# Score and value matmuls of two attention heads on alternating halves of the TensorE array

## The chip, the cores and the metric

The kernel runs on one core of one Trainium2 chip. The metric is the device time of the whole program in microseconds, from its first to its last instruction with the launch around it; lower is better. The chip has a TensorE (matrix engine, 128 x 128 array, "PE" in the profile, its weight loads "PEld"), VectorE ("DVE"), ScalarE ("ACT"), GpSimd ("POOL") and SyncE ("SP", which here issues DMA transfers).

## The reference

A two-layer decoder trunk on one sequence of 512 tokens with 1024 channels, float32. The part that matters here is the token mixing between two feed-forward blocks:

```python
h = rms_norm(x, mix_norm[i])
z = h @ w_in[i]
qkv_shape = (Bn, S, A_N_GROUPS, A_HEADS_PER_GROUP, HEAD_DIM)
q = z[..., Q_OFF:K_OFF].reshape(qkv_shape)
...
y_a = dilated_attention_mixture(q, k, v)
...
gates = jax.nn.sigmoid(z[..., G_OFF:] + b_gate[i]).reshape(Bn, S, N_BRANCH, D)
merged = (gates[:, :, 0] * (y_a @ w_proj_a[i])
          + gates[:, :, 1] * (y_b @ w_proj_b[i])
          + gates[:, :, 2] * (y_c @ w_proj_c[i]))
x = x + merged @ w_out[i]
```

There are 3 groups of 4 heads with 64 channels each. `dilated_attention_mixture` is a masked softmax attention per group, with the groups of one head slot mixed by their softmax denominators, which is one softmax over the keys of all three. Group 0 of a head looks back 128 tokens, group 1 at every 4th and group 2 at every 16th token. The kernel takes the tokens of one residue modulo 4 together, so one piece of attention is one head and one residue: 128 queries against 512 + 128 + 128 = 768 keys.

## The kernel before

**Projections.** Channels lie on the partitions, tokens in the free dimension. Each float32 product with a weight is made of three fp32r products, high by high, high by low and low by high. A "unit" is one block of a weight, 1024 rows by 256 columns. SyncE loads it into `raw`, ScalarE copies its high part to `w_hi` (L737), VectorE subtracts to get `w_lo` (L1030). There are two slots of each, so a unit is split while TensorE works on the one before it. One unit is 48 matmuls of 128 x 128 weights and 512 columns (2 column halves x 8 blocks x 3 products) into two banks of a PSUM pair, `psum0` or `psum1`. `columns` (L433) makes the units in a row.

**Attention phase.** It lies once in each layer, between the units of q and k for heads 0 and 1 and the merge of the three branches. It has 16 pieces of attention (4 heads x 4 residues) and, between them, 6 whole units: three for q and k of heads 2 and 3, three for the first three gates. The order is written out by hand in a loop over 18 slots: in a slot TensorE does the scores of the next piece, 8 projection matmuls (`part`, L444), the transposes of this piece, 8 more projection matmuls, and the values of this piece. Slots 0 and 9 have no piece of their own; before the scores in slot 9, TensorE waits until VectorE has taken the unit that held q and k of heads 2 and 3.

- `scores` (L619): three plain float32 matmuls of 64 rows (one head's channels, partitions 0 to 63 or 64 to 127) by 128 columns of weights against 512, 128 and 128 keys, into `side0`. The trace shows each float32 matmul as two, each with its own load.
- VectorE adds the mask and takes the row maximum (L1340, L1344), ScalarE takes the exponential (L941), VectorE divides (L1349, L1350).
- `transposes` (L629): six blocks of 128 x 128 into `side1`, copied by ScalarE to `pT` (L963).
- `values` (L641): six float32 matmuls of 128 rows by 64 columns of weights against 128 columns, summed into partitions 0 to 63 or 64 to 127 of the last 128 columns of `side1`. ScalarE copies the high part (`head_hi`, L926), VectorE subtracts the low part (`head_lo`, L1329).

All 4 residues of head 0 come first, then those of head 1, and so on, so that pieces in a row use the same half of the array.

**Merge.** `project` multiplies ya (2 blocks), yb (4) and yc (4) by 256 columns of their weights, in the order a, b, c; VectorE multiplies each with its gate and adds (L1392 to L1403). Three gate units of the next 256 columns stand before each following `project`.

Of the kernel before, what the change touches and what calls it, by code (L numbers as in the profile page):

```python
# [18 lines left out]
F32 = mybir.dt.float32  # L19
# [56 lines left out]
def trunk(nc, x, ffn1_norm, ffn1_w_gate, ffn1_w_up, ffn1_w_down, mix_norm, w_in, b_gate, b_ln_g,  # L76
# [16 lines left out]
    ATT = HEADS * RES  # L93
    KEYS = S + 2 * P
# [5 lines left out]
    EV0, EV1 = 47, 47  # L100
# [4 lines left out]
    with ExitStack() as ctx:  # L105
# [48 lines left out]
        pT = at("pT", M + 42 * KB_, KEYS)  # L154
# [52 lines left out]
        unit_done = sem("unit_done")  # L207
        evacuated = [sem(f"evacuated{s}") for s in range(2)]
# [43 lines left out]
        SLOTS = 18  # L252
# [7 lines left out]
        OUT_BANKS = (2, 1, 0, 1)  # L260

        def attended(s):

            if s in (0, 9) or not 0 < s < SLOTS:
                return None
            return s - 1 if s < 9 else s - 2
# [6 lines left out]
        def _(sp):  # L273
# [40 lines left out]
            with rounds(sp, DEPTH, counts, split_made=UNITS_PER_LAYER) as layer:  # L314
# [83 lines left out]
        def _(pe):  # L398
# [39 lines left out]
            def part(dst, w, x_hi, x_lo, q0, q1):  # L438

                whi, wlo = w  # L440
                for q in range(q0, q1):
                    c, k, n = q // (3 * KD), q // 3 % KD, q % 3
                    l, r = ((whi, x_hi), (whi, x_lo), (wlo, x_hi))[n]
                    mm = nc.tensor.matmul(dst[:, c * S:(c + 1) * S], l[:, k * UNIT_N + c * P:k * UNIT_N + (c + 1) * P],  # L444
                                          r[:, k * S:(k + 1) * S], start=(k == 0 and n == 0), stop=(k == KD - 1 and n == 2))
                return mm

# [70 lines left out]
            with rounds(pe, DEPTH, counts, unit=UNITS_PER_LAYER, ev0=EV0, ev1=EV1,  # L518
                        sv0=8 + ATT, sv1=4, h=3 * D_PAIRS, acc=3 * (1 + KD), act=2 * FF_UNITS, w_sT=1, pooled=4,
                        vb=1, p=ATT, pT=ATT, head=ATT, y=2, merged=D_PAIRS) as layer:  # L520
# [88 lines left out]
                def scores(n):  # L609
                    j, r = divmod(n, RES)  # L610
                    rows_ = slice((j % 2) * HEAD_DIM, (j % 2 + 1) * HEAD_DIM)
                    t = qk[j // 2]
                    o = begin_side(0)
                    col = 0
                    for g in range(GROUPS):
                        q, k = g * S + r * P, (GROUPS + g) * S
                        keys = t[rows_, k:k + S] if g == 0 else t[rows_, k + r * P:k + (r + 1) * P]
                        width = S if g == 0 else P
                        mm = nc.tensor.matmul(o[:, col:col + width], t[rows_, q:q + P], keys, start=True, stop=True)  # L619
                        col += width  # L620
                    mm.then_inc(side_done[0], 1)

                def transposes(n):

                    pe.wait_ge(p_made, counts["p"].next())

                    pe.wait_ge(head_made, counts["head"].next())
                    for c in range(KEYS // P):
                        mm = nc.tensor.transpose(side[1][:, c * P:(c + 1) * P], p_tile[n % 2][:, c * P:(c + 1) * P], ident[:, :])  # L629
                    mm.then_inc(pT_written, 1)  # L630

                def values(n):
                    j, r = divmod(n, RES)

                    pe.wait_ge(pT_made, counts["pT"].next())
                    out_rows = slice((j % 2) * HEAD_DIM, (j % 2 + 1) * HEAD_DIM)
                    o = side[1][out_rows, KEYS:KEYS + P]
                    for c in range(KEYS // P):
                        g, t = (0, c) if c < TILES else (c - TILES + 1, r)
                        col = t * A_WIDTH + g * A_OUT + j * HEAD_DIM  # L640
                        mm = nc.tensor.matmul(o, v[:, col:col + HEAD_DIM], pT[:, c * P:(c + 1) * P],  # L641
                                              start=(c == 0), stop=(c == KEYS // P - 1))
                    mm.then_inc(head_done, 1)

                pair_of = (0, 1, 0, 1, 0, 1)
                STEP = 3 * 2 * KD // 6
                for s in range(SLOTS):
                    m, third = divmod(s, 3)
                    this, after = attended(s), attended(s + 1)
                    if third == 0:  # L650
                        o = begin(pair_of[m])
                        w = unit()
                    if this is not None and after is not None:
                        scores(after)

                    start, end = 2 * STEP * third, 2 * STEP * (third + 1)
                    before, between = (STEP, STEP) if s < SLOTS - 1 else (STEP // 2, STEP - 2)
                    part(o, w, h_hi, h_lo, start, start + before)
                    if this is None:
                        if s == 0:  # L660

                            pe.wait_ge(side_evacuated[1], counts["sv1"].now(1))

                        pe.wait_ge(evacuated[1 - pair_of[m]], counts[f"ev{1 - pair_of[m]}"].now(1))
                        scores(after)
                    else:
                        transposes(this)
                    mm = part(o, w, h_hi, h_lo, start + before, start + before + between)
                    if third == 2 and s < SLOTS - 1:
                        mm.then_inc(unit_done, 1)  # L670
                    if this is not None:
                        values(this)
                part(o, w, h_hi, h_lo, start + before + between, end).then_inc(unit_done, 1)

                def project():
                    columns(begin(0), unit(), ya_hi, ya_lo, range(KA), True, True).then_inc(unit_done, 1)
                    columns(begin(1), unit(), yb_hi, yb_lo, range(KB), True, True).then_inc(unit_done, 1)
                    columns(begin(0), unit(), yc_hi, yc_lo, range(KB), True, True).then_inc(unit_done, 1)  # L680
                pe.wait_ge(head_made, counts["head"].now(1))
                pe.wait_ge(y_ready, counts["y"].next(2))
                project()
                with rounds(pe, D_PAIRS - 1, counts, unit=6, ev0=3, ev1=3):
                    for s in (1, 0, 1):
                        columns(begin(s), unit(), h_hi, h_lo, range(KD), True, True).then_inc(unit_done, 1)
                    project()
# [36 lines left out]
        def _(act):  # L724
# [105 lines left out]
            with rounds(act, DEPTH, counts, unit=UNITS_PER_LAYER, raw0=8 * UNITS_PER_LAYER + 16 * 2,  # L830
                        raw1=8 * UNITS_PER_LAYER + 16 * 3, ev0=EV0, ev1=EV1, se0=8 + ATT, act=2 * FF_UNITS,
                        sd0=7 + ATT, sd1=4, ln=1, yb=2, neg=ATT, pT_written=ATT, head=ATT, merged=D_PAIRS) as layer:
# [84 lines left out]
                counts["sd0"].next(ATT)  # L917
# [3 lines left out]
                def head_hi(n):  # L921
                    j, r = divmod(n, RES)
                    rows_ = slice((j % 2) * HEAD_DIM, (j % 2 + 1) * HEAD_DIM)
                    act.wait_ge(head_done, counts["head"].next())
                    dst = ya_hi[rows_, (j // 2) * S:(j // 2 + 1) * S].rearrange("p (i r) -> p r i", r=RES)[:, r, :]
                    nc.scalar.activation(dst, side[1][rows_, KEYS:KEYS + P],  # L926
                                         ACT.Copy).then_inc(ya_hi_made, 1)
# [10 lines left out]
                def exponential(n):  # L938

                    act.wait_ge(neg_max_made, counts["neg"].next())  # L940
                    nc.scalar.activation(p_tile[n % 2][:, :], p_tile[n % 2][:, :], ACT.Exp, bias=neg_max[:, n % 2:n % 2 + 1],  # L941
                                         accum_out=row_sum[:, n % 2:n % 2 + 1]).then_inc(exp_made, 1)

                bias_col = T_BGATE + layer * (3 * KD)
                next_unit = [dict(parts=2), dict(parts=2), {}, {}, {}, dict(k=KA)]
                for s in range(SLOTS):
                    m, third = divmod(s, 3)
                    if attended(s - 1) is not None:
                        head_hi(attended(s - 1))
                    if third == 0:  # L950
                        if m > 0:
                            counts["unit"].next()
                            if m - 1 < 3:
                                counts[f"ev{(m - 1) % 2}"].next()
                        split(**next_unit[m])
                    if third == 1 and m > 3:
                        sigmoids(m - 4, (m - 1) % 2, bias_col)
                    if third == 1 and m > 3:

                        exponential(attended(s + 1))  # L960
                    if attended(s) is not None:
                        act.wait_ge(pT_written, counts["pT_written"].next())
# [495 lines left out]
```

## Time and profile before

| | |
|---|---|
| median of 3 runs | 2417.64 us (2417.22 to 2418.68) |
| the profiled execution's own time | 2416.66 us |
| its span, first to last instruction | 2414.9 us |
| mean granted TensorE clock | 0.997 of full speed |
| busy: TensorE, its loads, VectorE, ScalarE, GpSimd | 2394.2, 1969.6, 1095.0, 716.6, 30.5 us |
| attention phase of layer 0, from its first projection matmul to the last one | 525.59 to 655.24 us |
| attention phase of layer 1 begins | 1715.33 us |

The busy time says which engine is full. The chain that ended last says, step by step, which instruction each next one waited for. The groups by line give how many of a kind there are and how long one takes; matmuls are pipelined, so the mean of one is longer than the distance between two starts, and the distance is what counts.

### The profile page before, as it was taken

The page shows a single profiled execution, that of the slowest core. Times are in us where ns is not written, and L with a number is a line of the kernel's source. Part 1 is how long each engine was busy: PE and PEld are TensorE (multiplying, and loading weights), DVE is VectorE, ACT ScalarE, POOL GpSimd, SP SyncE. Part 2 cuts the span into 40 slices and gives each one's busy share as a digit, 9 for nine tenths or more (in the row PEclk, how much of TensorE's full clock was granted, in tenths as well). Part 3 has the DMA queues.
Part 4 walks back from the last instruction along what each step waited for, and adds up shares of the span by engine and source line. Part 5 has one row for each costly group of instructions (what it writes and reads, how often), then busy time and mean ns, then how long its engine had stood idle before and what let it go on. Part 6 is the DMA issues. An engine that isn't in the chain of part 4 may idle for free.

```text
span 2414.9 us, 27466 instructions
## 1 busy us (share of the span) xinstructions
PE 2394.2 (99%) x11021; PEld 1969.6 (82%) x11021; DVE 1095.0 (45%) x1045; ACT 716.6 (30%) x665; POOL 30.5 (1%) x58
## 2 busy tenths in 40 slices
PE   7999999999999999999999999999999999999999
PEld 6888888887788888888888888888777888888887
DVE  7444435544454554443344443365544445544433
ACT  4222223323422332222232222232334223322222
POOL 4000000000000000000000000000000000000000
PEclk9999999999999999999999999999999999999999
DMA  4333223321132323322332332332312233232221
GB/s 141 94 97 104 81 98 122 95 81 40 40 104 87 114 89 102 104 89 95 96 101 91 104 100 84 96 116 79 88 31 66 83 109 109 91 104 91 96 96 65
DMA packets 229756, 221.81 MB, mean 92 GB/s; under 512 B 4161, under 2 KB 227505, under 8 KB 229681
## 3 DMA queue, kind: packets, MB, share of 16 engines
q1 hardware_dynamic: 225696, 215.29, 28.4%
q10 hardware_dynamic: 3984, 5.51, 0.7%
q8 instruction: 48, 0.79, 0.1%
q14 instruction: 28, 0.22, 0.0%
HBM read 218.69 MB, written 2.10 MB: 91 GB/s over the span
## 4 chain that ended last, share of the span: by engine, by line
PE 97%; ACT 1%; DVE 1%; issue 0%; DMA 0%; ACTq 0%; DVEq 0%
PE psum L433 83%; PE psum L444 5%; PE side L641 2%; PE psum L561 2%; PE side L619 2%; PE side L433 1%; PE psum L453 1%; PE side L629 1%; DVE acc L1087 0%; PE side L571 0%; PE side L543 0%; DMA x_in<-in_x_dram 0%; ACT gate L934 0%; PE side L582 0%; ACT L941 0%
## 5 line engine op out<-in xcount | busy, mean ns | idle before, releaser
L433 PE MATMUL psum<-h_hi,w_hi 128*128 128x512 f32 x1984 | 776.0, 391 | 8.7 <-DVE w_lo L1030 8.5
L433 PE MATMUL psum<-h_lo,w_hi 128*128 128x512 f32 x1984 | 772.8, 390 | 0.0
L433 PE MATMUL psum<-h_hi,w_lo 128*128 128x512 f32 x1984 | 772.7, 389 | 0.0
L1030 DVE TENSOR_TENSOR w_lo<-raw,w_hi 128x2048 fp32r<-128x2048 f32 (+2 forms) x224 | 470.9, 2102 | 338.5 <-ACT w_hi L737 337.8
L737 ACT ACTIVATE w_hi<-raw 128x2048 fp32r<-128x2048 f32 (+2 forms) x224 | 393.8, 1758 | 601.9 <-PE psum L433 578.1
L433 PEld LDWEIGHTS psum<-h_hi,w_hi 128*128 128x128 f32 x1984 | 373.0, 188 | 88.5 <-issue 9.2
L433 PEld LDWEIGHTS psum<-h_hi,w_lo 128*128 128x128 f32 x1984 | 373.0, 188 | 77.9
L433 PEld LDWEIGHTS psum<-h_lo,w_hi 128*128 128x128 f32 x1984 | 373.1, 188 | 77.7 <-issue 1.2
L433 PE MATMUL psum<-act_hi,w_hi 128*128 128x512 f32 x704 | 273.9, 389 | 0.0
L433 PE MATMUL psum<-act_lo,w_hi 128*128 128x512 f32 x704 | 273.9, 389 | 0.0
L433 PE MATMUL psum<-act_hi,w_lo 128*128 128x512 f32 x704 | 273.9, 389 | 0.0
L793 ACT ACTIVATE act_hi<-us 128x1024 f32 (+1 forms) x44 | 46.7, 1061 | 455.0 <-DVE us L1118 455.0
L1052 DVE TENSOR_TENSOR us<-psum,rstd 128x1024 f32<-128x1024 f32 x44 | 53.9, 1225 | 276.5 <-PE psum L433 276.5
L433 PEld LDWEIGHTS psum<-act_hi,w_lo 128*128 128x128 f32 x704 | 132.2, 188 | 27.5
L433 PEld LDWEIGHTS psum<-act_lo,w_hi 128*128 128x128 f32 x704 | 132.2, 188 | 27.5
L433 PEld LDWEIGHTS psum<-act_hi,w_hi 128*128 128x128 f32 x704 | 132.2, 188 | 27.2
L1052 DVE TENSOR_TENSOR gs<-psum,rstd 128x1024 f32<-128x1024 f32 x44 | 53.9, 1225 | 119.4 <-PE psum L433 118.9
L1120 DVE TENSOR_TENSOR act_lo<-us,act_hi 128x1024 f32 (+1 forms) x44 | 53.9, 1226 | 58.7 <-ACT act_hi L793 58.7
L755 ACT ACTIVATE us<-xT 128x1024 f32<-128x1024 f32 x24 | 25.4, 1059 | 185.1 <-DVE xT L1065 185.1
L444 PE MATMUL psum<-h_hi,w_hi 128*128 128x512 f32 x192 | 77.8, 405 | 0.0
L444 PE MATMUL psum<-h_hi,w_lo 128*128 128x512 f32 x192 | 77.7, 405 | 0.0
L444 PE MATMUL psum<-h_lo,w_hi 128*128 128x512 f32 x192 | 77.4, 403 | 0.0
(185 smaller groups left out, 1942.4 us busy)
## 6 DMA issues: line engine op xcount, KB each, us to landing
raw<-in_ffn_w_gate_dram SPq DMA_DIRECT2D x44, 1024.0 KB, 5.3
raw<-in_ffn_w_up_dram SPq DMA_DIRECT2D x44, 1024.0 KB, 5.3
raw<-in_w_in_dram SPq DMA_DIRECT2D x42, 1024.0 KB, 5.3
raw<-in_ffn_w_down_dram SPq DMA_DIRECT2D x32, 1024.0 KB, 4.9
raw<-in_ffn_w_down_dram SPq DMA_DIRECT2D x16, 768.0 KB, 4.2
raw<-in_w_in_dram SPq DMA_DIRECT2D x24, 512.0 KB, 4.4
raw<-in_w_out_dram SPq DMA_DIRECT2D x8, 1024.0 KB, 5.0
raw<-in_w_proj_b_dram SPq DMA_DIRECT2D x8, 512.0 KB, 3.4
```

What stands on the lines that cost most here:

```text
L433: mm = nc.tensor.matmul(dst[:, c * S:(c + 1) * S], l[:, a], r[:, b], start=first and k == ks[0] and n == 0, stop=last and k == ks[-1] and ...
L444: mm = nc.tensor.matmul(dst[:, c * S:(c + 1) * S], l[:, k * UNIT_N + c * P:k * UNIT_N + (c + 1) * P], r[:, k * S:(k + 1) * S], start=(k == ...
L453: mm = nc.tensor.matmul(o, l[:, k * P:(k + 1) * P], r[:, k * S:(k + 1) * S], start=(k == 0 and n == 0), stop=(k == KD - 1 and n == 2))
L561: mm = nc.tensor.matmul(d, l[:, k * S + t * P:k * S + (t + 1) * P], r[:, b], start=(k == 0 and m == 0), stop=(k == KD - 1 and m == 2))
L619: mm = nc.tensor.matmul(o[:, col:col + width], t[rows_, q:q + P], keys, start=True, stop=True)
L641: mm = nc.tensor.matmul(o, v[:, col:col + HEAD_DIM], pT[:, c * P:(c + 1) * P], start=(c == 0), stop=(c == KEYS // P - 1))
L737: nc.scalar.activation(w_hi[s][:, 0:k * n], raw[s][:, 0:k * n], ACT.Copy).then_inc(hi_made, 1)
L755: nc.scalar.activation(sq[:, :], pair(xT, d), ACT.Square).then_inc(sq_made, 1)
L793: nc.scalar.activation(pair(act_hi, i), us[:, :], ACT.Copy).then_inc(act_hi_made, 1)
L1030: nc.vector.tensor_tensor(w_lo[s][:, a], raw[s][:, a], w_hi[s][:, a].bitcast(F32), ALU.subtract).then_inc(split_made, 1)
L1052: return nc.vector.tensor_tensor(dst, two(psum[s][:, :]), rstd2, ALU.mult)
L1120: nc.vector.tensor_tensor(pair(act_lo, i), us[:, :], pair(act_hi, i).bitcast(F32), ALU.subtract).then_inc(act_ready, 1)
```

## The change

- The 16 pieces become 8 pairs: heads 0 and 1 (then 2 and 3) of one residue. `score_pair` issues the three score matmuls of both heads in turn: rows 0 to 63 into `side0`, rows 64 to 127 into `psum1`, which the phase no longer needs for projections. `value_pair` issues the six value matmuls of both heads in turn, to partitions 0 to 63 and 64 to 127 of the same columns of `side1`, with two tiles `pT`.
- `turn_pair` transposes the first head into `side1` and the second into `side0`; ScalarE copies both.
- All six units go through `psum0`, a half (24 matmuls, one bank) at a time; VectorE takes a half as soon as it is done (`take_half`). The places of the scores and of the transposes in the stream of 288 projection matmuls are two tables. The values of a pair follow on the scores of the next pair.
- `head_hi` and `head_lo` take both heads at once (128 partitions, 8 times a layer instead of 16).
- In the merge the order is b, a, c, with the PSUM pairs exchanged, and TensorE waits for the last head's output only before the a unit. SyncE loads the weights in that order.

The core of the diff:

```diff
+        SCORES_AT = (10, 48, 86, 124, 162, 194, 226, 258)
+        TURNS_AT = (38, 76, 114, 152, 185, 217, 249, 281)
-                    for w in (w_proj_a, w_proj_b, w_proj_c):
+                    for w in (w_proj_b, w_proj_a, w_proj_c):
...
+                def project_to(end):
+                    for q in range(stream["at"], end):
+                        h, k, n = q // (3 * KD), q // 3 % KD, q % 3
+                        c = h % 2
+                        if q % (3 * KD) == 0:
+                            pe.wait_ge(evacuated[0], free + max(h - 1, 0))
+                            if c == 0:
+                                stream["w"] = unit()
...
+                def score_pair(n):
+                    jp, r = divmod(n, RES)
+                    t = qk[jp]
+                    outs = (begin_side(0), begin(1))
+                    if n == RES:
+                        pe.wait_ge(evacuated[0], free + 6)
                     for g in range(GROUPS):
...
+                        for b in range(2):
+                            mm = nc.tensor.matmul(outs[b][:, col:col + k1 - k0], t[rows_of(b), q:q + P], t[rows_of(b), k0:k1],
+                                                  start=True, stop=True)
...
+                def value_pair(n):
+                    jp, r = divmod(n, RES)
+                    pe.wait_ge(pT_made, counts["pT"].next())
+                    pe.wait_ge(side_evacuated[0], counts["sv0"].now(1 if n == PAIRS - 1 else 0))
                     pe.wait_ge(head_made, counts["head"].next())
                     for c in range(KEYS // P):
                         g, t = (0, c) if c < TILES else (c - TILES + 1, r)
+                        for b in range(2):
+                            col = t * A_WIDTH + g * A_OUT + (2 * jp + b) * HEAD_DIM
+                            mm = nc.tensor.matmul(side[1][rows_of(b), KEYS:KEYS + P], v[:, col:col + HEAD_DIM],
+                                                  pT[b][:, c * P:(c + 1) * P], start=(c == 0), stop=(c == KEYS // P - 1))
...
+                for n in range(PAIRS):
+                    project_to(SCORES_AT[n])
+                    score_pair(n)
+                    if n > 0:
+                        value_pair(n - 1)
+                    project_to(TURNS_AT[n])
+                    turn_pair(n)
+                project_to(PHASE)
+                value_pair(PAIRS - 1)
...
+                for n in range(PAIRS):
+                    if n == 0:
+                        step(parts=2)
+                    if n > 0:
+                        head_hi(n - 1)
+                    if n == 1:
+                        step(parts=2)
+                    if n == 5:
+                        step()
+                    for b in range(2):
+                        exponential(b)
+                    if n in (2, 3):
+                        step()
+                    if n == 6:
+                        step(KB)
+                    take_turned()
+                    if n in (5, 6):
+                        counts["ev0"].next()
+                        sigmoids(n - 5, 0, bias_col)
```

TensorE in the attention phase before: the end of one slot's projection matmuls, the values of a piece, the scores of the next (`qk_87`: q and k of heads 0 and 1), and on.

```order
L444 MATMUL psum<-h_lo,w_hi_55 128x512
L641 MATMUL side<-pT,v 64x128 [waits pT_made]
L641 MATMUL side<-pT,v 64x128 x5
L410 REGISTER_ALU
L619 MATMUL side<-qk_87 128x512 [waits side_evacuated0]
L619 MATMUL side<-qk_87 128x128 x2
L444 MATMUL psum<-h_hi,w_lo_57 128x512
```

The same place now: the scores of one pair, behind them the values of the pair before (`pT_94` and `pT_95` are the two heads' tiles), then projection matmuls.

```order
L405 REGISTER_ALU [waits side_evacuated0]
L634 MATMUL side<-qk_87 128x512 [waits evacuated1]
L634 MATMUL psum<-qk_87 128x512
L634 MATMUL side<-qk_87 128x128
L634 MATMUL psum<-qk_87 128x128
L634 MATMUL side<-qk_87 128x128
L634 MATMUL psum<-qk_87 128x128
L663 MATMUL side<-pT_94,v 64x128 [waits head_made,side_evacuated0,pT_made]
L663 MATMUL side<-pT_95,v 64x128
L663 MATMUL side<-pT_94,v 64x128
L663 MATMUL side<-pT_95,v 64x128
```

What moved: heads alternate from one matmul to the next, and the values stand behind the scores instead of ahead of them. Eight value matmuls more follow.

ScalarE now, at the sixth pair: the split of a unit (`w_hi`) ahead of both exponentials, the two copies of the transposed tiles, then the sigmoids of a gate with their table load, ahead of the next pair's output and exponentials.

```order
L927 ACTIVATE ya_hi<-side 128x128 [waits head_done]
L736 REGISTER_ALU
L738 REGISTER_ALU [waits raw_loaded0]
L739 ACTIVATE w_hi_54<-raw_52 128x2048 [waits unit_done]
L940 REGISTER_ALU
L941 ACTIVATE p_tile_92,small<-p_tile_92,small 128x768 [waits neg_max_made]
L940 REGISTER_ALU
L941 ACTIVATE p_tile_93,small<-p_tile_93,small 128x768 [waits neg_max_made]
L946 ACTIVATE pT_94<-side 128x768 [waits pT_written]
L948 ACTIVATE pT_95<-side 128x768 [waits pT_written]
L932 REGISTER_ALU
L934 ISA [waits evacuated0]
```

Before, the exponential of a piece stood behind the copy of the piece before it; now both exponentials of a pair stand ahead of the copies of their own pair.

## Rows read from the trace of the kernel before

**Rows 1.** the page: busy time of each engine over the run

```profile
PE 2394.2 (99%) x11021; PEld 1969.6 (82%) x11021; DVE 1095.0 (45%) x1045; ACT 716.6 (30%) x665; POOL 30.5 (1%) x58
```

**Rows 2.** the page: the chain that ended last, by engine and line

```profile
PE psum L433 83%; PE psum L444 5%; PE side L641 2%; PE psum L561 2%; PE side L619 2%; PE side L433 1%; PE psum L453 1%; PE side L629 1%; DVE acc L1087 0%; PE side L571 0%; PE side L543 0%; DMA x_in<-in_x_dram 0%; ACT gate L934 0%; PE side L582 0%; ACT L941 0%
```

**Rows 3.** stretches: TensorE in the two attention phases, us, busy (count), clock

```profile
525.60:653.64 128.04, 126.65 (x667) 1.00 0.14 44
1715.33:1843.40 128.07, 126.67 (x668) 1.00 0.15 44
```

**Rows 4.** chain through one slot: start us, us, engine, tile, line

```profile
538.42 1.50 PE side L619 x6
539.92 2.04 PE psum L444 x8
541.96 0.66 PE side L629 x6
542.61 1.84 PE psum L444 x8
544.45 1.46 PE side L641 x12
```

**Rows 5.** the chain where layer 0's phase begins, turns and ends

```profile
525.59 1.81 PE psum L444 x8
...
590.23 2.01 DVE qk L1309 x2
...
655.24 64.94 PE psum L433 x286
```

**Rows 6.** groups of layer 0's phase: busy us, mean ns | idle before

```profile
L444 PE MATMUL psum<-h_hi,w_hi 128*128 128x512 f32 x96 | 38.9, 405 | 0.0
...
L619 PE MATMUL side<-qk 64*128 64x128 f32 (+1 forms) x96 | 25.1, 394 | 1.0 <-DVE qk L1309 1.0
L641 PE MATMUL side<-pT,v 128*64 128x128 f32 x192 | 24.4, 277 | 0.4 <-ACT pT L963 0.3
...
L926 ACT ACTIVATE ya_hi<-side 64x128 fp32r<-64x128 f32 x16 | 6.3, 392 | 26.6 <-PE side L641 26.6
```

**Rows 7.** waits of TensorE there: us in total, times, longest

```profile
PE side L619 <- DVE qk L1309: 1.0, 1, 1.0
PE side L641 <- ACT pT L963: 0.3, 1, 0.3
```

**Rows 8.** time order, TensorE in a value group (1, 3, 12 passes)

```profile
544.38 0.32 PE L641 MATMUL side<-pT,v 128*64 128x128 f32 x1
...
544.38 0.54 PE L641 MATMUL side<-pT,v 128*64 128x128 f32 x3
...
544.38 1.52 PE L641 MATMUL side<-pT,v 128*64 128x128 f32 x12
```

**Rows 9.** time order, loads of a score group, first projection matmul behind

```profile
546.37 0.19 PEld L619 LDWEIGHTS side<-qk 64*128 64x128 f32 x1 [0.24 <-issue]
...
546.80 0.30 PEld L619 LDWEIGHTS side<-qk 64*128 64x128 f32 x2 [0.24 <-issue]
...
612.39 0.50 PE L444 MATMUL psum<-h_hi,w_hi 128*128 128x512 f32 x1
```

**Rows 10.** time order, VectorE and ScalarE behind a score group

```profile
554.93 0.95 DVE L1340 CUSTOM_DVE_ANT_0 p_tile<-side,masks 128x768 f32<-128x768 f32 x1 [0.71 <-issue]
...
559.58 0.62 DVE L1350 TENSOR_SCALAR p_tile<-p_tile,small 128x768 f32<-128x768 f32 x1
...
557.62 0.81 ACT L963 ACTIVATE pT<-side 128x768 f32<-128x768 f32 x1 [3.80 <-PE side L629]
558.33 0.93 ACT L941 ACTIVATE p_tile<-p_tile,small 128x768 f32<-128x768 f32 x1
```

**Rows 11.** time order, ScalarE: a split, a table load

```profile
611.18 1.92 ACT L737 ACTIVATE w_hi<-raw 128x2048 fp32r<-128x2048 f32 x1
...
618.89 1.28 ACT L934 ACT_TABLE_LOAD   x1
```

More of the change, by code:

```diff
@@ L93, in trunk @@
     ATT = HEADS * RES
+    PAIRS = ATT // 2
     KEYS = S + 2 * P
@@ L436, in columns @@
                 return mm
[L438 to L446, printed above, removed]
             def one_column(o, w):
@@ new lines, in turn_pair @@
+                def turn_pair(n):
+                    pe.wait_ge(p_made, counts["p"].next())
+                    if n == 0:
+                        pe.wait_ge(side_evacuated[1], counts["sv1"].now(1))
+                    for c in range(KEYS // P):
+                        mm = nc.tensor.transpose(side[1][:, c * P:(c + 1) * P], p_tile[0][:, c * P:(c + 1) * P], ident[:, :])
+                    mm.then_inc(pT_written, 1)
+                    pe.wait_ge(p_made, counts["p"].next())
+                    o = begin_side(0)
+                    for c in range(KEYS // P):
+                        mm = nc.tensor.transpose(o[:, c * P:(c + 1) * P], p_tile[1][:, c * P:(c + 1) * P], ident[:, :])
+                    mm.then_inc(pT_written, 1)
@@ L632, in values @@
[L632 to L638, printed above, removed]
-                        g, t = (0, c) if c < TILES else (c - TILES + 1, r)
[L640 to L672, printed above, removed]
@@ new lines, in _, with project @@
+                for n in range(PAIRS):
[7 more added lines that the diff above has]
+                value_pair(PAIRS - 1)
+                def project(last_head=False):
+                    columns(begin(1), unit(), yb_hi, yb_lo, range(KB), True, True).then_inc(unit_done, 1)
+                    if last_head:
+                        pe.wait_ge(head_made, counts["head"].now(1))
@@ L678, in project @@
                     columns(begin(0), unit(), ya_hi, ya_lo, range(KA), True, True).then_inc(unit_done, 1)
-                    columns(begin(1), unit(), yb_hi, yb_lo, range(KB), True, True).then_inc(unit_done, 1)
-                    columns(begin(0), unit(), yc_hi, yc_lo, range(KB), True, True).then_inc(unit_done, 1)
-                pe.wait_ge(head_made, counts["head"].now(1))
+                    columns(begin(1), unit(), yc_hi, yc_lo, range(KB), True, True).then_inc(unit_done, 1)
                 pe.wait_ge(y_ready, counts["y"].next(2))
-                project()
+                project(True)
@@ L921, in head_hi @@
                 def head_hi(n):
[L922 to L927, printed above, removed]
+                    jp, r = divmod(n, RES)
+                    act.wait_ge(head_done, counts["head"].next(2))
+                    dst = ya_hi[:, jp * S:(jp + 1) * S].rearrange("p (i r) -> p r i", r=RES)[:, r, :]
+                    nc.scalar.activation(dst, side[1][:, KEYS:KEYS + P], ACT.Copy).then_inc(ya_hi_made, 1)
                 def sigmoids(g, s, col):
@@ L946, in _ @@
[L946 to L962, printed above, removed]
-                        nc.scalar.activation(pT[:, :], side[1][:, 0:KEYS], ACT.Copy).then_inc(pT_made, 1)
-                    if attended(s + 1) is not None and not (third == 1 and m > 3):
-                        exponential(attended(s + 1))
@@ L966, in _, with take_turned @@
-                head_hi(ATT - 1)
-                counts["unit"].next()
+                    nc.scalar.activation(p_tile[b][:, :], p_tile[b][:, :], ACT.Exp, bias=neg_max[:, b:b + 1],
+                                         accum_out=row_sum[:, b:b + 1]).then_inc(exp_made, 1)
+                def take_turned():
+                    act.wait_ge(pT_written, counts["pT_written"].next())
+                    nc.scalar.activation(pT[0][:, :], side[1][:, 0:KEYS], ACT.Copy).then_inc(pT_made, 1)
+                    act.wait_ge(pT_written, counts["pT_written"].next())
+                    nc.scalar.activation(pT[1][:, :], side[0][:, 0:KEYS], ACT.Copy).then_inc(side_evacuated[0], 1)
@@ L1383, in _ @@
-                head_lo(ATT - 1)
-                done()
-                take_gate(2, 1)
+                        evac(0, take_qk(1, QK_UNITS[m][c], 0, c))
+                    else:
+                        evac(0, nc.vector.tensor_tensor(gate[m - 3][:, c * S:(c + 1) * S], psum[0][:, c * S:(c + 1) * S],
+                                                        rstd[:, :], ALU.mult))
+                for n in range(PAIRS):
+                    score_max(n)
+                    if n > 0:
+                        head_lo(n - 1)
+                    normalise(0)
+                    normalise(1)
+                    if n < 4:
+                        take_half((0, 2, 3, 5)[n])
+                        split()
+                        if n in (0, 2):
+                            take_half((1, None, 4)[n])
+                    elif n in (4, 7):
+                        take_half(6 if n == 4 else 10)
+                        take_half(7 if n == 4 else 11)
+                    elif n == 5:
+                        split()
+                        take_half(8)
+                    else:
+                        take_half(9)
+                        split(KB)
```

170 lines of the change are left out of this document (83 added, 87 removed).

## The prediction

> **What bounds the kernel now.** I read first the busy times of the page, then its chain of work, then the stretches of the attention phases, one slot of the chain, the groups and waits of that phase, and last single instructions in order of time. TensorE is busy 99% of the span [rows 1], and 83% of the chain are its projection matmuls outside the attention phase, which the change leaves alone [rows 2]. So time can only come from TensorE's own work or from its few idle gaps. In the two attention phases it is busy for 126.65 and 126.67 us of 128 at a granted clock of 1.00, which is the 2.4 GHz level [rows 3]. VectorE and ScalarE work there too, but TensorE waits for them only twice in layer 0: 1.0 us for q and k in slot 9 and 0.3 us for a copy behind a sigmoid [rows 7].
>
> One slot takes 7.50 us: scores 1.50, 8 projections 2.04, transposes 0.66, 8 projections 1.84, values 1.46 [rows 4]. Two readings matter. First, 8 projections cost 0.20 us more behind scores than behind transposes: TensorE pays about 0.2 us when it changes between the whole array and half of it. It pays the like in front of values and between values and scores: twelve value passes take 1.52 us from first start to last end, three take 0.54 us, so the passes are (1.52 - 0.54) / 9 = 0.109 us apart [rows 8], 1.31 us for twelve, and 1.46 us holds 0.15 us of change. In the scores the long passes are 546.80 - 546.37 = 0.43 us apart [rows 9]; with two long and four short passes of 0.11 us that is 1.30 us, and 1.50 holds 0.20 us of change. Second, every pass of a group now uses the same half of the array, and each load is issued when the pass ahead of it starts (the two load rows are those 0.43 us apart [rows 9]), never two ahead.
>
> **The change, part by part**, per layer. The stretch before goes from 525.59 to 655.24 us [rows 5], 129.65 us: 16 scores x 1.50 = 24.0, 16 values x 1.46 = 23.4, 16 transposes x 0.66 = 10.6, 288 projections (three kinds of 96 [rows 6]) as 36 eights, half at 2.04 and half at 1.84, = 69.8, waits 1.3; 129.1 in all, 0.5 us unassigned.
>
> *Without any overlap*, the new order costs: 288 projections x 0.230 (1.84 / 8) = 66.2; 8 changes back behind the values x 0.20 = 1.6; 16 transposes = 10.6; 8 score pairs x (1.50 + 1.30) = 22.4, since the second head needs no change; 8 value pairs x (1.46 + 1.31) = 22.2. Sum 123.0, so 6.6 us less per layer, 13.3 us in two. This counts the old waits as gone: the 1.0 us because the first scores of heads 2 and 3 stand at projection 162 while the last of their halves is done at 144, 18 x 0.23 = 4.1 us earlier, against 2.01 us for both halves of a unit [rows 5]; the 0.3 us because the sigmoids no longer stand ahead of a copy.
>
> *Overlap of the two halves.* No row of before shows two halves at work at once, so I bound it. The floor of the gain is nothing. The other end: a pass of one head runs together with the preceding head's second pass. Each float32 matmul is two passes, and those two use the same half, so they can't overlap each other. A score pair then takes 3 long and 4 short slots, 3 x 0.43 + 4 x 0.11 = 1.73 us in place of 4 x 0.43 + 8 x 0.11 = 2.60; a value pair takes 13 slots of 0.109 in place of 24, 1.42 in place of 2.62. That is 2.07 us per pair and 33.1 us over 16 pairs. A middle case: the load of the other half isn't issued until the pass ahead of it has started, as all loads in the trace. A load that nothing covers costs about 0.10 us for 128 columns (the first projection behind scores is 0.50 us long, its group's mean is 0.405 [rows 6, 9]) and 0.05 us for 64 columns (first value pass 0.32 against a mean of 0.277 [rows 6, 8]). Stepping through the passes with 0.11 and 0.055, a score pair takes 2.04 us and a value pair 6 x (2 x 0.109 + 2 x 0.055) = 1.97 us: 1.21 us per pair, 19.4 us in all. The trace can't tell these two apart, because the loads it shows go to the half whose spare weights are already taken; I take their middle, 26 us.
>
> The Trainium skill (TensorE: Matmul & The Clock Gate, Part 3, the mechanism) says that a weight load overlaps matmuls in flight only when the row group differs. Our rows speak against the strict form: value loads use all rows and still start with the pass ahead. By the rule the score pair gets its full overlap and the value pair gets none, and the sum would be the second rival's below.
>
> *Other engines.* The mask, maximum, exponential and division are as many as before. Behind the end of a score pair (e) VectorE needs 0.95 us per head plus the negation, so the second maximum is ready at about e + 2.4. ScalarE must first copy the previous pair's output, after the values (about e + 2.1, then 0.39 us [rows 6]); two exponentials of 0.93 us bring e + 4.5, and the division of 0.62 us e + 5.3 [rows 10]. TensorE reaches the transposes only after 23 projections, 5.3 us, at about e + 7.4. The cover is 2 us. A split of 1.92 us ahead of the exponentials (second and sixth pair) or a table load of 1.28 us (seventh, eighth) [rows 11] uses it nearly up, but the second head's tile is needed 0.66 us later still. The two copies of 0.81 us [rows 10] start while the second half of the transposes runs and end about 1.2 us behind it; 9 projections give 2.1 us. If this cover is gone, each late pair puts its lateness on TensorE directly. Taking halves instead of units, one copy and one subtraction per pair instead of two, all lie beside TensorE. SyncE issues the same loads, two in another order. In the merge the matmul count is the same and TensorE never waits in it before; the new order lets the last head's output arrive during the b unit, which I count within the 0.5 us above.
>
> **Sum.** 13.3 + 26.2 = 39.5 us off the profiled execution's 2416.66 us (span 2414.9 and 1.8 around it) is 2377.2; the median of the runs is 1.0 us above that execution, so **2378 us**. The ends of the overlap give 2371 and 2385.
>
> **The rivals.**
> 1. *The halves don't overlap at all* (the change does not do what it says for float32). For it: nothing in the trace shows overlap. Against: the halves share no rows or columns and write different banks or partitions. Only the 13.3 us stay: 2404 us. Chance 0.13.
> 2. *Only the scores overlap*, by 0.87 us x 16 = 13.9 us: value loads for the other half wait, since both use all rows. Against: value loads already run beside passes. 2417.6 - 13.3 - 13.9 = 2390 us. Chance 0.12. It is what the Trainium skill's rule above (the same page and section) would give.
> 3. *Waits take the gain back.* Without overlap, 13.3 / 16 = 0.83 us of lateness per pair at the transposes brings the old time; the covers above speak against more than a few such pairs. 2415 to 2418 us. Chance 0.04.
> 4. *Slower: alternating costs what a change of the array costs.* If going from one half to the other drained TensorE as the change to the whole array does, 0.20 us, a pair with 5 alternations in the scores and 11 in the values would pay 3.2 us, 16 pairs 51 us: 2404 + 51 = 2455 us. It decides from 13.3 / 256 = 0.05 us per alternation. For it: before never alternates within a group. Against: both halves are the same shape of array, and the changes that the rows price are all between shapes. Chance 0.05.
>
> **How the numbers follow.** The overlap in both kinds has 0.66 and spans 2371 to 2385; with a few us of unassigned time on either side 2366 is the low end. Main case and rival 2 are 0.78, so the range must reach rival 1 at 2404. A measurement of this kernel tells 0.2%, about 5 us, from no change: faster by more holds the main case and rivals 1 and 2, 0.91; within it rival 3, 0.04; slower rival 4, 0.05.
>
> **What would show it.** In the profile after, the attention phase should last about 110 us (129.65 - 6.6 - 16.5 = 106.5 at full overlap, 113 with loads one ahead, 123 with none). In order of time, a score pair's first pass of the second head should start before the first head's second pass ends; value passes should stand about 0.06 to 0.08 us apart instead of 0.109. The 0.2 us behind values should be there 8 times. Waits of TensorE for p_tile or pT of over 1 us in all would show the cover wrong; passes further apart than 0.109 us, rival 4. A clock below 1.00 in the phase would be a thing I did not foresee.

## The result, and the profile after

| | before | changed |
|---|---|---|
| median | 2418.16 us (2417.22 to 2418.83, 4 runs) | 2363.05 us (2362.69 to 2363.96, 4 runs) |
| span of the profiled execution | 2414.9 us | 2362.2 us |
| TensorE busy | 2394.2 us | 2344.6 us |
| attention phase of layer 0 | 525.59 to 655.24, 129.65 us | 526.80 to 628.35, 101.55 us |

The ratio of the two is 0.9773, 95% interval 0.9756 to 0.979: 55 us faster. The four times of before are the three of the first table and one more. The prediction was 2378 us, faster, in a range from 2366 to 2404 us. The direction was right, the gain was 40% larger than forecast and the time lies 3 us below the range.

The page of the changed kernel, busy times and granted clock:

```profile
PE 2344.6 (99%) x11021; PEld 1939.8 (82%) x11021; DVE 1090.0 (46%) x1035; ACT 707.8 (30%) x649; POOL 27.9 (1%) x58
...
PEclk9999999999999999999999999999999999999999
```

The stretches of TensorE in both attention phases, changed kernel (us, busy (count), clock, DMA share, GB/s):

```profile
526.80:628.35 101.55, 101.55 (x673) 1.00 0.18 55
1689.29:1790.84 101.55, 101.55 (x674) 1.00 0.18 55
```

Before, the phase took 129.65 us in layer 0 [rows 5] and 129.66 us in layer 1 (1715.33 to 1844.99 in the chain). Both are now 28.1 us shorter. The clock is still full, and the profile shows no wait of TensorE in them: the 1.3 us of [rows 7] are gone.

The chain of the changed kernel through the end of one pair and the next, to hold against [rows 4]:

```profile
540.77 0.62 PE side L634
541.40 0.01 PE psum L634
541.40 0.42 PE side L634
...
542.28 1.46 PE side L663 x24
543.74 6.59 PE psum L616 x28
550.32 0.66 PE side L645 x6
```

The values of two heads, 24 passes, take 1.46 us, as long as the 12 passes of one head before. The scores of two heads go from 540.77 to 542.28, 1.51 us (1.50 in other pairs), as long as those of one head before. So both heads ran at the same time, from the first pass to the last. Single instructions show it. Time order on TensorE in the first part of that score group, changed kernel (start us, us):

```profile
540.70 0.69 PE L634 MATMUL side<-qk 64*128 64x512 f32 x1
540.71 0.69 PE L634 MATMUL psum<-qk 64*128 64x512 f32 x1
541.24 0.59 PE L634 MATMUL side<-qk 64*128 64x512 f32 x1
541.24 0.59 PE L634 MATMUL psum<-qk 64*128 64x512 f32 x1
541.67 0.27 PE L634 MATMUL side<-qk 64*128 64x128 f32 x1
541.67 0.27 PE L634 MATMUL psum<-qk 64*128 64x128 f32 x1
```

`side` is the first head, `psum` the second. Within one head the second pass starts 0.54 us behind the first and the third 0.43 us behind the second (540.70, 541.24, 541.67), as one head alone does, and the other head's pass starts within 0.01 us of each. The loads too run together, the same stretch with the loads shown:

```profile
541.24 0.19 PEld L634 LDWEIGHTS side<-qk 64*128 64x128 f32 x1 [0.23 <-issue]
...
541.25 0.19 PEld L634 LDWEIGHTS psum<-qk 64*128 64x128 f32 x1
```

### The profile page after: what moved, and what is told of

It is laid out like the page before. It is cut to its first block, busy times and chain, and to the rows that moved or that the text cites. A ratio compares the mean times of both kernels' runs of the same rounds, so it can differ in the third digit from the quotient of the medians.

```text
span 2362.2 us, 27568 instructions
## 1 busy us (share of the span) xinstructions
PE 2344.6 (99%) x11021; PEld 1939.8 (82%) x11021; DVE 1090.0 (46%) x1035; ACT 707.8 (30%) x649; POOL 27.9 (1%) x58
## 4 chain that ended last, share of the span: by engine, by line
PE 98%; DVE 1%; ACT 0%; DMA 0%; issue 0%; ACTq 0%; DVEq 0%
PE psum L432 84%; PE psum L616 6%; PE psum L550 2%; PE side L634 1%; PE side L663 1%; PE side L432 1%; PE psum L442 1%; PE side L650 0%; PE side L645 0%; DVE acc L1094 0%; PE side L560 0%; PE side L532 0%; DMA x_in<-in_x_dram 0%; PE side L571 0%; DVE h_lo L1085 0%; PE side L455 0%
```

## The experiments

Ten kernels were timed in three groups, each with the kernel before beside them. It took 2417.82 us beside the first group (scores in blocks, values in blocks, same rows, values two and two), 2416.76 beside the second (values three and three, little overlap, values apart, wait first) and 2417.09 beside the last (mixed merge order, and the changed kernel again, 2362.69). The first group is compared with the changed kernel's 2363.05 us. In the second the changed kernel did not run; 55.1 and 54.4 us less than before, the two differences that were measured, put it at 2361.7 to 2362.4 us. Differences there are taken from 2362.4 and can be 0.7 us larger. Each diff is against the changed kernel.

**Scores in blocks**

```diff
-                    for g in range(GROUPS):
+                    for b in range(2):
+                        for g in range(GROUPS):
...
-                        for b in range(2):
```

> The changed kernel with the score matmuls of a pair in blocks: three of the first head, then three of the second; nothing else moved. Theory A (TensorE starts matmuls in issue order and two neighbours on different halves run side by side, both passes of each): only the last matmul of the first head has a neighbour on the other half, so a score pair costs 0.86 + 0.22 + 1.30 = 2.38 us in place of 1.30, 1.08 us more; 16 pairs 17.3 us, 2380 us in all. Theory B (TensorE looks past a blocked matmul, and the second head's matmuls overtake): no change, 2363 us. Theory C (the gain did not come from overlap but from the other moves): no change, 2363 us.

Measured: 2378.66 us, 15.6 us more than the changed kernel. That is near theory A, and theories B and C are out as they were put. But the single instructions contradict A's first words, that TensorE starts matmuls in issue order. Time order on TensorE in a score group of this kernel (`x3` are three passes in a row):

```profile
540.93 1.23 PE L634 MATMUL side<-qk 64*128 64x512 f32 x3
541.90 0.69 PE L634 MATMUL psum<-qk 64*128 64x512 f32 x1
542.00 0.49 PE L634 MATMUL side<-qk 64*128 64x128 f32 x3
542.43 1.03 PE L634 MATMUL psum<-qk 64*128 64x512 f32 x5
```

In the program all six passes of the first head (`side`) stand ahead of the second head's (`psum`). Yet after three of them a pass of the second head starts, and the last three of the first head only start behind it, from 542.00. So TensorE does not start matmuls strictly in the program's order: a pass whose half is free went ahead of three waiting passes of the other half. The block's price follows: the group takes 541.00 to 543.46 in the chain, 2.46 us in place of 1.50, and 16 x 0.96 = 15.4 us. It is also the sum of the two long passes that the second head starts behind the first, 2 x 0.43 us, and of the 0.10 us of its first load, which nothing covers: its second pass starts 0.53 us behind its first (541.90, 542.43) instead of 0.43.

```profile
541.00 1.16 PE side L634 x3
542.16 0.11 PE psum L634
542.27 0.22 PE side L634 x2
542.50 0.97 PE psum L634 x5
543.46 1.46 PE side L663 x24
```

**Values in blocks**

```diff
-                    for c in range(KEYS // P):
-                        g, t = (0, c) if c < TILES else (c - TILES + 1, r)
-                        for b in range(2):
+                    for b in range(2):
+                        for c in range(KEYS // P):
+                            g, t = (0, c) if c < TILES else (c - TILES + 1, r)
```

> The changed kernel with the value matmuls of a pair in blocks, six of the first head and then six of the second. Theory A (issue order, neighbours on different halves side by side): 11 slots of 2 x 0.109 us in place of 6, 1.09 us more per pair, 17.4 us over 16 pairs, 2380.5 us. Theory B (the second head's overtake) and theory C (no overlap behind the gain): 2363 us.

Measured: 2378.41 us, 15.4 us more. The chain of this kernel has the value pair at 2.39 us:

```profile
541.20 2.39 PE side L663 x24
```

That is 0.93 us more than 1.46. The names of the tiles don't tell the heads apart here, but the starts do: 0.109 us apart up to the ninth pass at 542.05, and the next one already at 542.06. The passes under way at 542.22 and at 542.33 on TensorE, the start of the oldest in front:

```profile
542.05 0.44 PE L663 MATMUL side<-pT,v 128*64 128x128 f32 x4
542.06 0.54 PE L663 MATMUL side<-pT,v 128*64 128x128 f32 x5
```

So the second head starts beside the first head's ninth pass, ahead of the last three, just as in the scores. It is eight passes late, 8 x 0.109 = 0.87 us, and its first load, which nothing covers, adds 0.05 us. Theory A had it start beside the eleventh, 1.09 us late, and so came out 2 us too high.

**Same rows for both heads**

```diff
-                            mm = nc.tensor.matmul(outs[b][:, col:col + k1 - k0], t[rows_of(b), q:q + P], t[rows_of(b), k0:k1],
+                            mm = nc.tensor.matmul(outs[b][:, col:col + k1 - k0], t[rows_of(0), q:q + P], t[rows_of(0), k0:k1],
```

> The changed kernel, but the second head's scores are made from the first head's q and k (rows 0 to 63 for both), so the second head of each pair is left out and the order, the banks and the waits stay. If the gain of the pairs hangs on the two halves of the rows: no overlap in the scores, 1.30 us more per pair, 20.8 us in all, 2384 us. If alternating between two PSUM banks is what made it faster: no change, 2363 us.

Measured: 2384.45 us, 21.4 us more, as the two halves demand (20.8 was expected). Same order, same banks, same waits, and every pass now waits for the one ahead. The chain of this kernel in one score pair shows the order of the passes too, two of one matmul and then two of the other head's:

```profile
542.20 1.05 PE side L634 x2
543.26 0.86 PE psum L634 x2
544.11 0.22 PE side L634 x2
544.34 0.22 PE psum L634 x2
544.56 0.22 PE side L634 x2
544.78 0.22 PE psum L634 x2
```

2.81 us for the pair, 1.31 more than 1.50, and 16 x 1.31 = 21.0. For the scores, then, the overlap comes from the halves of the array, not from alternating banks.

**Values two and two**

```diff
-                    for c in range(KEYS // P):
+                    for c, b in [(2 * i + e, b) for i in range(KEYS // P // 2) for b in range(2) for e in range(2)]:
```

> The changed kernel with the value matmuls in the order two of the first head, two of the second, two of the first, and so on. Theory A: five of the boundaries still set neighbours side by side, 7 slots of 0.218 us in place of 6: 0.22 us more per pair, 3.5 us in all, 2366.5 us. Theory B (overtaking): 2363 us. A rival, that neighbours overlap only where alternation goes on without a break: 12 slots, 1.3 us more per pair, 2384 us.

Measured: 2364.14 us, 1.1 us above the changed kernel, which is no more than executions of one kernel differ by; theory A's 3.5 us are not there. Value pair 1.51 us against 1.46, which would be 0.8 us in all. Two matmuls are four passes; once the first has started, three wait, and the second head's go ahead of those three. The order in which the matmuls are written matters little up to there. The third rival is out by 20 us.

```profile
541.50 1.51 PE side L663 x24
```

**Values three and three**

```diff
-                    for c in range(KEYS // P):
+                    for c, b in [(3 * i + e, b) for i in range(KEYS // P // 3) for b in range(2) for e in range(3)]:
```

> The changed kernel with the value matmuls in the order three of the first head, three of the second, and again. Theory A (issue order, only neighbours on different halves side by side): three of twelve matmuls overlap, 9 slots of 0.218 us in place of 6, 0.65 us more per pair, 10.5 us over 16 pairs, 2373.5 us. Theory B' (a pass may start ahead of up to three waiting passes of the other half, as the blocks of scores and of values showed): the second head starts two passes late at the start of the group and keeps that distance, 14 passes of 0.109 us in place of 12, 0.22 us per pair, 3.5 us in all, 2366.5 us; the second head's first pass should stand 0.27 us behind the first head's first one.

Measured: 2368.08 us beside 2416.76 before, 5.7 us above the changed kernel's place there. The chain has the value pair at 1.73 us:

```profile
541.20 1.73 PE side L663 x24
```

That is 0.27 us more than 1.46, so 16 x 0.27 = 4.3 us. It is the start that had been expected: the second head's first pass stands 0.28 us behind the first head's (541.41 and 541.13), beside the third pass, which is two passes of 0.109 us and 0.05 us of a first load that nothing covers. Theory A had 0.65 us. The rest of the 5.7 us is near what executions of this kernel differ by. The rule with three waiting passes held in a case that it had not been made from; whether it counts passes, loads or both was not tried.

**Little overlap**

```diff
-                            mm = nc.tensor.matmul(outs[b][:, col:col + k1 - k0], t[rows_of(b), q:q + P], t[rows_of(b), k0:k1],
+                            mm = nc.tensor.matmul(outs[b][:, col:col + k1 - k0], t[rows_of(0), q:q + P], t[rows_of(0), k0:k1],
...
-                        for b in range(2):
+                    for b in range(2):
+                        for c in range(KEYS // P):
```

> The changed kernel with both overlaps taken away as far as it goes: the second head's scores come from the first head's q and k (the second head of each pair is left out), and the values stand in blocks of six. If the two effects add up: 2363.05 + 21.4 (scores on the same rows) + 15.4 (values in blocks) = 2399.8 us, and with the three value passes per pair that still overlap (3 x 0.109 x 16 = 5.2 us) a kernel without any overlap would take 2405 us, against the 2404 us that the prediction worked out for the new order alone. If one overlap hides a wait that the other then shows, more: over 2402 us.

Measured: 2399.56 us beside 2416.76, 37.2 us above the changed kernel's place, where 21.4 + 15.4 = 36.8 had been measured one by one: the effects add up. Part of the overlap is still in it, and more than the expectation's 5.2 us. Value pairs take 2.38 us in this kernel's chain; with no overlap they would take 1.46 + 1.31 = 2.77, so 16 x 0.39 = 6.2 us are left, and the new order alone stands at about 2405.8 us. That is 11 us below the 2416.76 beside it, where the forecast had 13.3. The whole overlap is worth 2405.8 - 2362.4 = 43 us by the times and 16 x (1.30 + 1.31) = 42 us by the chains.

**Values apart from the scores**

```diff
                     if n > 0:
+                        project_to(SCORES_AT[n] + 2)
                         value_pair(n - 1)
```

> The changed kernel with two projection matmuls moved between the scores of a pair and the values of the pair before. If each change of the array's shape costs about 0.2 us, this adds one such change 7 times a layer, 14 times in all: 2.2 to 2.8 us more, about 2365.5 us. If the shape costs nothing and the 0.2 us behind scores and values is something else (the end of the group itself), no change: 2363 us.

Measured: 2365.78 us beside 2416.76, 3.4 us more for 14 places, 0.24 us each, against the 0.2 us that [rows 4] had given; executions differ by too much to tell the two apart. The chain of this kernel:

```profile
541.50 0.67 PE psum L616 x2
542.18 1.46 PE side L663 x24
```

Two projection matmuls take 0.67 us where 0.46 us (2 x 0.23) is their work. The 0.2 us is the price of a change between the array's shapes. It isn't the end of any group of float32 matmuls: behind the transposes, which use the whole array, [rows 4] has none of it. The Trainium skill (TensorEngine Tiling (Array Packing), Key Properties) says that a change of tiling mode drains TensorE while a change of tile does not; this trace agrees on both, with 0.2 us for the one and 0.01 us or less between the halves for the other.

**Wait for the last pair first**

```diff
                 def project(last_head=False):
-                    columns(begin(1), unit(), yb_hi, yb_lo, range(KB), True, True).then_inc(unit_done, 1)
                     if last_head:
                         pe.wait_ge(head_made, counts["head"].now(1))
+                    columns(begin(1), unit(), yb_hi, yb_lo, range(KB), True, True).then_inc(unit_done, 1)
```

> The changed kernel, but TensorE waits for the last pair's output ahead of the b unit instead of ahead of the a unit: what the new merge order hides. The last values end, ScalarE copies 0.4 us and VectorE subtracts 0.4 us, with about 0.3 us of signals: TensorE idles some 1.1 us per layer, 2.2 us in all, 2365 us. If it is hidden anyway, 2363 us.

Measured: 2364.92 us beside 2416.76, 2.5 us more. The chain behind the last values leaves TensorE:

```profile
626.13 1.51 PE side L663 x24
627.64 0.02 issue
627.67 0.41 ACT ya_hi L927
628.07 0.02 issue
628.10 0.40 DVE ya_lo L1335
628.49 0.21 issue
628.71 11.48 PE psum L432 x49
```

1.07 us of idle TensorE per layer, 2.1 us in all, is what the b unit in front hides.

**Mixed merge order, and the changed kernel again**

```diff
+                    if last_head:
+                        columns(begin(1), unit(), yb_hi, yb_lo, range(KB), True, True).then_inc(unit_done, 1)
+                        pe.wait_ge(head_made, counts["head"].now(1))
+                        columns(begin(0), unit(), ya_hi, ya_lo, range(KA), True, True).then_inc(unit_done, 1)
+                    else:
+                        columns(begin(1), unit(), ya_hi, ya_lo, range(KA), True, True).then_inc(unit_done, 1)
+                        columns(begin(0), unit(), yb_hi, yb_lo, range(KB), True, True).then_inc(unit_done, 1)
```

(and the loads, splits and gates of VectorE and ScalarE in the same order).

> The changed kernel with the merge order b, a, c only for the first 256 columns, where it hides the last pair's output, and the old order a, b, c for the other three. In the trace of the changed kernel TensorE starts the c unit some 0.16 us late each time, since the low part of its weights and the a unit, the shortest, stand next to each other. If the order is the cause, three such places a layer go, 6 x 0.16 = 1.0 us less than the changed kernel beside it, about 2362 us, and the distance across the start of the c unit falls to 0.23 us. If the late start only moves to another unit, no change: 2363 us.

> The changed kernel once more, as it is, on the same chip as the run with the mixed merge order: 2363 us. It says how far two times of one call can be told apart, and how much the first 35 us and the last 15 us of the program differ from one execution to the next.

Measured: 2362.27 us (2361.68 to 2362.73, 5 runs) with the mixed order, 2362.69 us (2361.99 to 2364.98, 5 runs) for the changed kernel beside it; ratios to before 0.9773 (0.976 to 0.9787) and 0.9776 (0.9763 to 0.979). The difference of 0.4 us can't be told from nothing, nor from the 1.0 us that was expected. The traces do show the place. Changed kernel again, time order on TensorE and VectorE at the start of a c unit:

```profile
681.52 0.39 PE L432 MATMUL psum<-ya_hi,w_lo 128*128 128x512 f32 x1
681.80 0.50 PE L432 MATMUL psum<-yc_hi,w_hi 128*128 128x512 f32 x1
682.14 0.39 PE L432 MATMUL psum<-yc_lo,w_hi 128*128 128x512 f32 x1
...
679.39 1.22 DVE L1414 TENSOR_TENSOR gate<-gate,psum 128x1024 f32<-128x1024 f32 x1 [3.78 <-PE psum L432]
680.53 1.22 DVE L1037 TENSOR_TENSOR w_lo<-raw,w_hi 128x1024 fp32r<-128x1024 f32 x1
```

The a unit is the shortest, 12 matmuls or 2.7 us, and in its time VectorE must take the b product and make the low part of the c weights, 2 x 1.22 us. The c unit starts 0.05 us late and its next matmul another 0.11 us (0.28 and 0.34 us in place of 0.23). With the mixed order the distances are 0.23 us again, as expected:

```profile
682.20 0.39 PE L432 MATMUL psum<-yb_hi,w_lo 128*128 128x512 f32 x1
682.43 0.39 PE L432 MATMUL psum<-yc_hi,w_hi 128*128 128x512 f32 x1
682.66 0.39 PE L432 MATMUL psum<-yc_lo,w_hi 128*128 128x512 f32 x1
```

Some of the loads' waits for `w_lo` are now in front of the b unit (0.5 us in three, as in the kernel before), and no matmul starts late there. So the order is the cause of the late c units. What it is worth in time, the runs can't tell.

## Why the prediction was right or wrong, point by point

1. *TensorE is the bound, the phase is the place.* Right. All of the gain is in the two phases: 28.1 us in each, 56.2 in all. The spans differ by 52.7 us; 1.6 us went back between and behind the phases (1060.09 us from the end of the first to the start of the second before, 1060.94 after, and the like behind the second): the late c units, and the array change behind the last values, which now lies outside the phase. Some 1.2 us lie in the first 35 us of this execution; they don't belong to the change, since another execution of the changed kernel began its steady part where before did, at 33.38 us. The last 0.7 us lie at the end, where the granted clock was 0.59 over 5.5 us in the changed kernel's execution and 0.77 over 4.3 us in that of before, so partly at the 1.2 GHz level. In both, 5.2 us of 128-column matmuls (43 and 44 of them, TensorE busy for 4.94 and 4.99 us) came before at the full clock. The kernels have the same work there; that the difference is chance was not tried.
2. *New order without overlap, 13.3 us.* Right within some 2 us. By the traces, 28.1 us less 8 x 2.61 us of overlap leaves 7.2 us per layer, 14.4 in all, against 6.6 and 13.3 (the forecast had 0.5 us per layer unassigned); with the 1.6 us that went back behind the phases it is 12.8. By the run with little overlap it is 11.
3. *Overlap, 26.2 us.* This step failed, in its size. It said: "Each float32 matmul is two passes, and those two use the same half, so they can't overlap each other", and went on as if the second head's first pass had to wait until the first head's second pass had started. The first clause is right; the conclusion took starts in issue order for granted. The runs show in its place that a pass goes ahead of up to three waiting passes of the other half, so that the first passes of both heads run side by side and then the second ones. The overlap is whole: a pair gains 2.61 us, where the two cases of the forecast had 2.07 and 1.21, and the phase takes 101.55 us where full overlap was to give 106.5. In two layers that is 16 x (1.30 + 1.31) = 41.8 us in place of the 26.2 of the sum and of 33.1 at its upper end. 2417.6 - 13.3 - 41.8 = 2362.5 us, against 2363.05; that it comes so near is partly luck, since this sum leaves out the start and the end of the executions and the late c units. The upper end was no bound: the simple floor, both heads in the time of one, should have stood there.
4. *Loads one ahead.* Wrong across the halves: the loads of the two heads start 0.01 us apart and last as long as before. Within one half it still holds, each load starts with the pass ahead of it. I had read a rule for the whole array from loads that all went to one half.
5. *Rival 2, only the scores overlap.* Out: the values overlap as fully as the scores, with loads that use the same rows. The rule of the Trainium skill (TensorE: Matmul & The Clock Gate, Part 3, the mechanism) that a load overlaps only with another row group does not hold for the two column halves here, 24 passes in 1.46 us. The same section says that matmuls never start or end out of issue order; the scores in blocks show a start out of it.
6. *Rival 4, a change cost for each alternation.* Out, with 0.01 us or less between halves. *Rival 1*, out by 41 us. *Rival 3*, waits: none in either phase.
7. *The covers.* Right: TensorE waits nowhere. The forecast for a pair with a table load ahead of the exponentials was 2.1 us less 1.28, about 0.8 us. For the last pair of layer 0 (e = 617.06) VectorE ends the second division at 623.11, e + 6.1:

```profile
622.49 0.62 DVE L1366 TENSOR_SCALAR p_tile<-p_tile,small 128x768 f32<-128x768 f32 x1
```

TensorE begins the transposes at 623.96 in the chain, e + 6.9 instead of e + 7.4, since the values took 1.46 us. ScalarE could begin earlier for the same reason, so the cover is 0.85 us, and the second head's own transposes come 0.66 us later still.
8. *The merge.* I counted it within the 0.5 us that were unassigned, as TensorE never waited there before. That was about 1 us too little. The kernel before hid the last head's output behind its last six projection matmuls. The changed kernel has no projections left there; the b unit hides the 1.07 us a layer instead, so this is a cost that was avoided and no gain. What the new order adds are the late c units, three of 0.16 us and a first one of 0.09 us in a layer, about 1.2 us in two layers.

## What to carry to other kernels

When two groups of matmuls use opposite halves of the array, price the pair at the time of one and write them alternately, in runs of no more than two float32 matmuls per half. Keep all half-array work of a round together, since each change between a half and the whole array costs 0.2 us here, and put long whole-array work between the producer and the user of each tile. When bounding a gain that no row shows, let the far end be the physical floor, not a schedule that assumes an order of issue.

## What the hardware showed that I had not expected

- TensorE starts passes out of issue order across halves: three waiting passes were overtaken in the scores in blocks, and the times of the other orders (1.51 us at two and two, 1.73 at three and three, 2.39 at six and six, against 1.46 alternating) fit the same depth: none, two and eight passes of 0.109 us late, and each time 0.05 us for one load that nothing covers.
- Two halves by columns, which read different data on all 128 rows for weights and for moving data, run at full speed side by side: 24 float32 passes in 1.46 us.
